# Leaving out the zero matmuls ahead of two steps of the recurrent block

## The chip, the cores and the metric

The kernel runs on one core of a Trainium2 chip. The metric is device microseconds of one execution. The core has TensorE (PE; its weight loads are PEld), VectorE (DVE), ScalarE (ACT), GpSimd (POOL) and SyncE (SP, which issues the DMAs here). Each works through its own queue in order and waits for the others on semaphores.

## What is computed

A trunk of two layers over 256 tokens of width 1024, in float32. Each layer has a combined projection, windowed attention and RWKV-7 time mixing side by side, an output projection, a product-key expert block, and a gated embedding. The change touches the time mixing. Cut to what matters:

```python
def _rwkv7_mix(f, mu, w0, w_up, a0, a_up, g_up, k_k, k_a, r_k, lnx_w, lnx_b):
    ...
    w = -jax.nn.softplus(-(w0 + jnp.tanh(xw) @ w_up)) - 0.5
    decay = jnp.exp(-jnp.exp(w.astype(jnp.float32)))
    a = jax.nn.sigmoid(a0 + xa @ a_up)
    g = jax.nn.sigmoid(xg) @ g_up
    kk = (k * k_k).astype(jnp.float32).reshape(B, S, H, N)
    kk = kk / jnp.maximum(jnp.linalg.norm(kk, axis=-1, keepdims=True), 1e-12)
    k = k * (1.0 + (a - 1.0) * k_a)
    ...
    y = _rwkv7_scan(rh, hs(decay), kh, vh, -kk, kk * ah)
    ...
    bonus = jnp.sum(rh * kh * r_k.astype(jnp.float32), axis=-1, keepdims=True)

def reference(x, p, ...):
    for i in range(DEPTH):
        h = _rmsnorm(x, norm_mix[i])
        f = h @ w_in[i] + b_in[i]
        attn = _rmsnorm(_swa_sink_attention(...), attn_out_norm[i])
        rw = _rwkv7_mix(...)
        x = x + jnp.concatenate([attn, rw], axis=-1) @ w_out[i]
        x = x + _peer(_rmsnorm(x, norm_ffn[i]), peer_wq[i], peer_keys[i], peer_u[i], peer_v[i])
        gate = jax.nn.sigmoid(_rmsnorm(x, norm_ple[i]) @ ple_gate[i])
        x = x + (p[i] @ ple_proj[i]) * gate
    return _rmsnorm(x, norm_final)
```

`kk` is the key divided by its norm over the 64 channels of a head; `a`, `g` and the decay come from small (LoRA) projections.

## The kernel before, in words

Channels lie on partitions and tokens run along the free axis. In each of the two layers, TensorE does the 21 tiles of the input projection (`channel_rows`, L1250), with the attention's matmuls between them. Then it does, in this order of its queue:

1. eight transposes of the normed attention output `ao` (L1341);
2. `keep_warm(6, 4)`: four matmuls of a tile of zeros into PSUM bank 6 (L1238);
3. a wait for `sqk`, the squared scaled keys, which ScalarE makes (L512); then two matmuls with a matrix of ones per head, the key norms' sums (L1348);
4. the LoRA matmuls for decay and `a` (L1356, L1359), a wait for ScalarE's sigmoid of the gate input (L517), and the gate matmuls (L1364, L1365);
5. a wait for `rkprod` from VectorE (L906), and two matmuls with the ones, the bonus sums (L1371);
6. the transposes to token order (L1382) of `v` (`fm[:, 8:12]`), then `keep_warm(2, 4)` into bank 2, then a wait for the scaled keys `bt` and `kt` (VectorE, L914, L915), and their transposes;
7. a wait for `ar` (L917, L918) and `bonus_v` (L920) from VectorE; 16 products, one for each half of the tokens and head, each of two matmuls (L1395, L1396). VectorE copies each out of PSUM under a mask (`prods`, L925), and from the fifth on a product waits for the copy four before it;
8. six levels of a triangular inverse: products and transposes of 128x128 blocks (L1409, L1416, L1424), with masks from GpSimd (L375, L383).

Beside this, ScalarE makes the squares, the square root of the norms (`rnorm`, L516), the sigmoids (L522, L526), the copy of the gates `gT` (L529) and three exponentials (L532, L533, L535), the last of which `bt` waits for. VectorE takes the maximum of the sums (L890), the reciprocal (L892), scans (L896), and then `cprev`, `kmod`, `rkprod`, `kk`, `bvec`, `bt`, `kt`, `ar`, `bonus_v` in this order. The order of every engine is written out by hand.

A float32 matmul leaves two records in the trace, a transpose one. So four zero matmuls are eight records, and eight transposes are eight.

Of the kernel before, what the change touches and what calls it, by code (L numbers as in the profile page):

```python
# [105 lines left out]
def hybrid_encoder(nc, x, w_slabs, peer_slabs, vecs, consts, p_t, g_final, out):  # L106
    with ExitStack() as ctx:
# [6 lines left out]
        def place(name, at, shape, dt=F32):  # L114
            return nc.alloc_sbuf_tensor_at(name, [P] + shape, dt, offset=4 * (first + at))
# [6 lines left out]
        cst = place("cst", 14336, [NCONST])  # L122
# [10 lines left out]
        zeros = place("zeros", R + 25088, [P])  # L133
# [79 lines left out]
        PS = ctx.enter_context(nc.psum_tensor("PS", [P, 8, 512], F32))  # L213
# [1009 lines left out]
        def _(pe):  # L1223
            mm = pe.matmul
# [7 lines left out]
                        if tb == TB - 1 and k % 2:  # L1232
                            ins.then_inc(xT_ps, 1)

            def keep_warm(bank, n):

                for _ in range(n):
                    mm(PS[:, bank], zeros[:], cst[:, 0:512], start=True, stop=True)  # L1238

            def channel_rows(tile, dst, norm=None):  # L1240

                pe.wait_ge(low_pool if tile.by_pool else low_dve, tile.low + 1)
                b, n = tile.count % DEEP, 0
                for k in range(KT):
                    if norm is not None:

                        pe.wait_ge(hT_lo, KT * norm + k + 1)
                    ks = slice(k * P, (k + 1) * P)
                    for w, h in ((high, hTh), (high, hTl), (low, hTh)):
                        ins = mm(dst, w[:, b, ks], h[:, k], start=n == 0, stop=n == 3 * KT - 1)  # L1250
                        n += 1
                ins.then_inc(part_used, 1)
# [19 lines left out]
            for L in range(DEPTH):  # L1272
# [66 lines left out]
                for k in range(4):  # L1339
                    for tb in range(TB):  # L1340
                        ins = pe.transpose(PS[:, AOT_BANKS[k // 2], (k % 2) * SEQ + tb * P:(k % 2) * SEQ + (tb + 1) * P], ao[:, tb, k * P:(k + 1) * P], ident)  # L1341
                    if k % 2:
                        ins.then_inc(aoT_ps, 1)
                keep_warm(6, 4)

                pe.wait_ge(sqk_ready, L + 1)
                for n in range(2):
                    ins = mm(PS[:, 6 + n], ones2, sqk[:, 2 * n:2 * n + 2].rearrange("p a b -> p (a b)"), start=True, stop=True)  # L1348
# [26 lines left out]
                pe.wait_ge(g_ready, L + 1)  # L1375
                for n, src in enumerate((fm[:, 8:12], bt, kt)):
                    if n == 1:
                        keep_warm(2, 4)
                        pe.wait_ge(bkt_ready, 2 * L + 1)
                    for tb in range(TB):  # L1380
                        for t in range(4):
                            ins = pe.transpose(PS[:, 2 * n + tb, t * P:(t + 1) * P], src[:, t, tb * P:(tb + 1) * P], ident)  # L1382
                    ins.then_inc(tok_ps, 1)
# [44 lines left out]
                for c in range(NCHUNK):  # L1428
# [6 lines left out]
                    for t in range(4):  # L1435
                        if c:
                            mm(PS[rows, 0, t * P:(t + 1) * P], ar[:, t, tb, 0, cols], ST[:, (c - 1) % 2, t], start=True, stop=False)
                        for h in (2 * t, 2 * t + 1):
                            ins = mm(PS[rows, 0, h * HD:(h + 1) * HD], prods[:, tb * NH + h, 256 + o:256 + o + 64], vtok[:, tb, h * HD:(h + 1) * HD],
                                     start=c == 0, stop=c == 0 or h % 2 == 1)  # L1440
# [249 lines left out]
```

## Time and profile before

| | us |
|---|---|
| median of three timed runs | 2381.17 (2380.63 to 2383.16) |
| profiled execution, its own time | 2383.67 |
| its span, first to last instruction | 2381.9 |
| TensorE busy | 2255.2 |
| VectorE busy | 1670.5 |
| ScalarE busy | 1118.4 |
| GpSimd busy | 472.9 |
| mean granted TensorE clock | 0.974 of full speed |

The two stretches in which the changed lines run lie at about 90 to 133 us (layer 0) and 1273 to 1317 us (layer 1). Read each in three views: the chain of waits, which tells what ended last; the timeline of each engine, which tells when an input was ready; and the windows, which tell the granted clock (PEclk, 1.00 or 0.50 of full speed) in a stretch. A time of the timeline is the start of a group and its length; the last record of a matmul group overlaps the next group a little.

### The profile page before, as it was taken

Reading aid. Unit: us, or ns where it says so; the run is one execution under the profiler, and the core shown is the slowest. Engines: PE = TensorE matmul, PEld = TensorE weight load, DVE = VectorE, ACT = ScalarE, POOL = GpSimd, SP = SyncE. Lnnn points to the kernel's source line nnn. Section 1 sums busy time; section 2 is a strip of 40 time slices with the busy share of each in tenths; the row PEclk is TensorE's granted clock in tenths of the full one; section 3 lists DMA queues with packets and bytes.
Section 4 is the critical chain, followed back from the end, with each engine's and each line's share of the span. In section 5 each row is a group of like instructions: output and inputs, shape, how many; then the busy total and the mean of one; then the engine's idle time right before and its main releaser. Section 6 shows DMA issues by size and latency. Waiting matters only on the chain.

```text
span 2381.9 us, 51888 instructions
## 1 busy us (share of the span) xinstructions
PE 2255.2 (95%) x20000; PEld 2016.4 (85%) x20000; DVE 1670.5 (70%) x3044; ACT 1118.4 (47%) x1867; POOL 472.9 (20%) x206
## 2 busy tenths in 40 slices
PE   8898899999999999999898979999899999999997
PEld 7787889998888888788686978899888888887885
DVE  6754499697666676985567555987967666679754
ACT  5532455544444444445464324554444444454443
POOL 0040379840000000000000405797400000000000
PEclk9898899999999999999998989999999999999998
DMA  6201344533444444445342013344244444444451
GB/s 245 89 1 54 117 149 158 177 123 142 159 176 159 173 161 159 159 158 194 141 142 71 1 65 130 142 176 161 105 165 170 161 174 160 175 159 150 167 194 62
DMA packets 46601, 335.02 MB, mean 141 GB/s; under 512 B 5168, under 2 KB 5296, under 8 KB 6320
## 3 DMA queue, kind: packets, MB, share of 16 engines
q1 hardware_dynamic: 46512, 333.84, 39.3%
q8 instruction: 55, 0.90, 0.2%
q14 instruction: 34, 0.28, 0.0%
HBM read 332.77 MB, written 1.05 MB: 140 GB/s over the span
## 4 chain that ended last, share of the span: by engine, by line
PE 81%; DVE 6%; issue 5%; POOL 5%; ACT 2%; DMA 1%; SPq 0%; POOLq 0%; DVEq 0%; ACTq 0%
PE PS L1542 30%; PE PS L1519 24%; PE PS L1250 7%; PE PS L1531 6%; PE PS L1266 4%; POOL low L397 4%; PE PS L1409 2%; PE PS L1416 2%; DMA praw<-in_p_t 1%; DVE is_i L1090 1%; PE PS L1424 1%; PE PS L1238 1%; DVE rnorm L892 1%; PE PS L1282 0%; PE PS L1333 0%
## 5 line engine op out<-in xcount | busy, mean ns | idle before, releaser
L600 ACT CAST high<-ring 128x1024 fp32r<-128x1024 f32 x512 | 535.5, 1048 | 609.9 <-PE PS L1519 451.0
L1519 PE MATMUL PS<-hTh,high 128*128 128x256 f32 x2048 | 594.7, 290 | 13.9 <-ACT GA L604 11.9
L1519 PE MATMUL PS<-hTh,low 128*128 128x256 f32 x2048 | 578.5, 282 | 0.0
L1519 PE MATMUL PS<-hTl,high 128*128 128x256 f32 x2048 | 576.9, 282 | 0.0
L1027 DVE TENSOR_TENSOR low<-ring,high 128x1024 fp32r<-128x1024 f32 x384 | 457.2, 1219 | 0.3
L1519 PEld LDWEIGHTS PS<-hTh,high 128*128 128x128 f32 x2048 | 387.0, 189 | 18.9 <-ACT GA L604 9.7
L1519 PEld LDWEIGHTS PS<-hTl,high 128*128 128x128 f32 x2048 | 387.4, 189 | 0.0
L1519 PEld LDWEIGHTS PS<-hTh,low 128*128 128x128 f32 x2048 | 387.3, 189 | 0.0
L397 POOL TENSOR_TENSOR low<-ring,high 128x1024 fp32r<-128x1024 f32 x128 | 345.1, 2721 | 96.8 <-ACT high L600 96.6
L1542 PE MATMUL PS<-high,WH 128*128 128x512 f32 x1024 | 323.5, 397 | 0.0
L1542 PE MATMUL PS<-low,WH 128*128 128x512 f32 x1024 | 318.0, 392 | 0.0
L1542 PE MATMUL PS<-high,WL 128*128 128x512 f32 x1024 | 316.4, 390 | 0.0
L1090 DVE TENSOR_TENSOR is_i<-iota_half,repeats 128x256 bf16<-128x256 bf16 x256 | 135.3, 529 | 252.4 <-ACT repeats L630 251.2
L360 POOL TENSOR_SCALAR stat<-stat 128x1 f32<-128x1 f32 x14 | 4.7, 334 | 1502.6 <-ACT xn L430 1502.6
L1531 PEld LDWEIGHTS PS<-hot,hot 128*128 128x128 bf16 x6144 | 170.5, 96 | 69.0 <-issue 54.1
L1542 PEld LDWEIGHTS PS<-high,WL 128*128 128x128 f32 x1024 | 192.2, 188 | 43.0
L1542 PEld LDWEIGHTS PS<-low,WH 128*128 128x128 f32 x1024 | 192.2, 188 | 42.8
L1531 PE MATMUL PS<-hot,hot 128*128 128x32 bf16 x6144 | 195.3, 177 | 15.7 <-DVE hot L1097 15.7
L1542 PEld LDWEIGHTS PS<-high,WH 128*128 128x128 f32 x1024 | 178.9, 188 | 26.4
L621 ACT CAST WH<-GA 128x256 fp32r (+1 forms) x256 | 102.7, 401 | 201.5 <-PE PS L1542 191.0
L1093 DVE TENSOR_TENSOR hot<-iota_half,repeats 128x1024 bf16<-128x1024 bf16 x256 | 179.3, 700 | 0.0
L1250 PE MATMUL PS<-hTh,high 128*128 128x256 f32 x592 | 172.7, 292 | 3.8 <-DVE hTl L787 3.6
(251 smaller groups left out, 3305.4 us busy)
## 6 DMA issues: line engine op xcount, KB each, us to landing
ring<-in_peer_slabs SPq DMA_DIRECT2D x256, 1024.0 KB, 4.8
ring<-in_w_slabs SPq DMA_DIRECT2D x58, 1024.0 KB, 4.9
xres<-in_x SPq DMA_DIRECT2D x2, 512.0 KB, 4.7
out<-obuf SPq DMA_DIRECT2D x2, 512.0 KB, 2.6
cst<-in_consts SPq DMA_DIRECT2D x1, 904.0 KB, 12.1
praw<-in_p_t SPq DMA_DIRECT2D x1, 512.0 KB, 16.7
gfin<-in_g_final SPq DMA_DIRECT2D x1, 512.0 KB, 5.7
vec<-in_vecs SPq DMA_DIRECT2D x1, 356.0 KB, 8.4
```

What stands on the lines that cost most here:

```text
L397: pool.tensor_tensor(low[:, b], ring[:, place, half * D:(half + 1) * D], high[:, b].bitcast(F32), ALU.subtract).then_inc(low_pool, 1)
L600: act.copy(high[:, (c0[L] + j) % DEEP], ring[:, place, half * D:(half + 1) * D]).then_inc(part_hi, 1)
L621: act.copy(WH[:, j % 2:j % 2 + 1], GA[:, bass.ds(place, 1)]).then_inc(w_hi, 1)
L1027: dve.tensor_tensor(low[:, b], ring[:, place, half * D:(half + 1) * D], high[:, b].bitcast(F32), ALU.subtract).then_inc(low_dve, 1)
L1090: dve.tensor_tensor(is_i2[:, b].rearrange("p t (a c) -> p t a c", c=REP), iotas[:, QT // REP * chunk:QT // REP * (chunk + 1)].unsqueeze(1) ...
L1093: dve.tensor_tensor(hot1[:, b].rearrange("p t (a c) -> p t a c", c=REP), iotas.unsqueeze(1).broadcast_to([P, GROUP, NSUB // REP, REP]), re ...
L1250: ins = mm(dst, w[:, b, ks], h[:, k], start=n == 0, stop=n == 3 * KT - 1)
L1266: ins = mm(PS[:, bank0 + 2 * tb + s], h[:, k, tb * P:(tb + 1) * P], w[:, b, s * 512:(s + 1) * 512], start=first and k == 0 and c == 0, sto ...
L1409: ins = mm(PS[:, g, (n % 4) * P:(n % 4 + 1) * P], Mt[:, lv % 2, n], X[:, n] if lv else ident, start=True, stop=True)
L1519: ins = mm(PS[:, 6 + j % 2, 0:SEQ], u[:, b, ks], h[:, k], start=n == 0, stop=n == 3 * KT - 1)
L1531: ins = mm(PS[:, 4 + b, t * QT:(t + 1) * QT], hot1[:, b, t], hot2[:, b, part, t], start=part == 0, stop=part == 2)
L1542: ins = mm(PS[:, 2 * tb + s], w[:, j % 2, tb * P:(tb + 1) * P], v[:, b, s * 512:(s + 1) * 512], start=False, stop=False, skip_group_check= ...
```

## The change

The function `keep_warm` and its two calls are removed. Each call made four matmuls of zeros into a bank that the next real matmul writes afresh. No other line is changed: the waits, the order of the queues, the buffers and the tile `zeros` (which the expert block uses to open and close its accumulation) stay as they are.

```diff
-            def keep_warm(bank, n):
-
-                for _ in range(n):
-                    mm(PS[:, bank], zeros[:], cst[:, 0:512], start=True, stop=True)
-
...
-                keep_warm(6, 4)
-
                 pe.wait_ge(sqk_ready, L + 1)
...
                     if n == 1:
-                        keep_warm(2, 4)
                         pe.wait_ge(bkt_ready, 2 * L + 1)
```

## Rows read from the trace of the kernel before

**Rows 1.** The page: busy time of TensorE, and the chain that ended last, by engine
```profile
PE 2255.2 (95%) x20000; PEld 2016.4 (85%) x20000; DVE 1670.5 (70%) x3044; ACT 1118.4 (47%) x1867; POOL 472.9 (20%) x206
...
PE 81%; DVE 6%; issue 5%; POOL 5%; ACT 2%; DMA 1%; SPq 0%; POOLq 0%; DVEq 0%; ACTq 0%
```

**Rows 2.** Chain of waits, layer 0: start us, length us, what ran (x records)
```profile
92.08 3.44 PE PS L1238 x8
...
95.52 1.73 PE PS L1348 x4
...
113.89 3.41 PE PS L1371 x4
...
118.17 3.44 PE PS L1238 x8
...
121.61 1.75 PE PS L1382 x16
...
123.36 0.64 PE PS L1395 x4
```

**Rows 3.** Chain of waits, layer 1, same columns
```profile
1297.12 3.75 PE PS L1371 x4
...
1307.18 0.64 PE PS L1395 x4
...
1309.21 0.51 PE PS L1395 x2
```

**Rows 4.** Timeline of ScalarE: start us, us, engine, line, operation, tiles, count [idle before]
```profile
93.13 1.71 ACT L512 ACTIVATE sqk<-fm,vec 128x256 f32<-128x256 f32 x4
...
109.54 1.01 ACT L529 COPY gT<-PS 128x1024 f32<-128x1024 f32 x1 [5.09 <-PE PS L1365]
...
113.78 1.04 ACT L535 ACTIVATE wprev<-cprev 128x1024 f32<-128x1024 f32 x1
...
1291.79 1.01 ACT L529 COPY gT<-PS 128x1024 f32<-128x1024 f32 x1 [4.11 <-PE PS L1365]
```

**Rows 5.** Windows: us, busy (x) of PE, PEld, DVE, ACT, POOL; PEclk; DMA share, GB/s
```profile
97.25:100.13 2.88, 2.88 (x16) 2.25 (x16) 1.73 (x2) 1.58 (x2) 0.00 (x0) 1.00 0.00 0
...
103.17:109.51 6.34, 6.34 (x12) 2.49 (x10) 6.31 (x6) 1.28 (x4) 0.00 (x0) 0.50 0.00 0
...
138.02:140.49 2.47, 0.00 (x0) 0.00 (x0) 2.47 (x1) 0.00 (x0) 2.42 (x1) 1.00 0.00 0
...
140.72:144.13 3.41, 3.41 (x18) 3.41 (x18) 3.27 (x6) 0.59 (x1) 0.00 (x0) 0.50 0.00 0
...
1198.86:1202.20 3.34, 3.08 (x25) 3.09 (x25) 3.34 (x9) 1.81 (x5) 0.00 (x0) 1.00 0.90 314
```

**Rows 6.** Timeline of TensorE, layer 0: gate matmuls, and behind the products
```profile
101.58 0.70 PE L1364 MATMUL PS<-xg_s,ring 128*128 128x256 f32 x2 [1.45 <-ACT xg_s L517]
...
104.84 1.22 PE L1364 MATMUL PS<-xg_s,ring 128*128 128x256 f32 x2
...
134.21 3.81 PE L1409 MATMUL PS<-cst,Mt 128*128 128x128 f32 x32 [1.31 <-issue]
```

**Rows 7.** Timeline of VectorE, both layers: scaled keys, bonus, masked copies of products
```profile
116.17 1.23 DVE L914 TENSOR_TENSOR bt<-bvec,winv 128x1024 f32<-128x1024 f32 x1
...
117.32 1.22 DVE L915 TENSOR_TENSOR kt<-kmod,winv 128x1024 f32<-128x1024 f32 x1
...
120.72 1.22 DVE L920 TENSOR_TENSOR bonus_v<-PS,fm 128x1024 f32<-128x1024 f32 x1
...
124.45 9.65 DVE L925 TENSOR_TENSOR prods<-PS,cst 128x512 f32<-128x512 f32 x16 [2.51 <-PE PS L1396]
...
1303.95 1.22 DVE L920 TENSOR_TENSOR bonus_v<-PS,fm 128x1024 f32<-128x1024 f32 x1
```

**Rows 8.** Timeline of TensorE: transposes of the norm that opens layer 1
```profile
1194.77 1.97 PE L1231 MATMUL PS<-cst,xn 128*128 128x128 f32 x8 [6.99 <-DVE xn L781]
...
1196.91 1.97 PE L1231 MATMUL PS<-cst,xn 128*128 128x128 f32 x8 [0.17 <-DVE xn L781]
```

## The prediction

> **What bounds the kernel now.** I read the page first: TensorE is busy 95% of the span and the chain that ended last is 81% TensorE [rows 1]. A shorter TensorE program pays only where nothing else ends at the same moment, so the views of the two stretches decide, not the share. The removed work is 16 zero matmuls (two records each), four at each place in each layer, and the chain runs through them [rows 2]. In layer 0 it goes through the first four (92.08 to 95.52) and the sums at 95.52 into work of VectorE and ScalarE that ends in `rkprod`, then through the sums of `rkprod` at 113.89, the second zero matmuls (118.17 to 121.61) and 16 transposes to the products at 123.36 [rows 2]. Layer 1 repeats this 1183.23 us later up to the sums of `rkprod` (1297.12 against 113.89), its products starting at 1307.18 [rows 2, 3]. So both places are on the path. What matters is what is late next once they are gone, and what TensorE's clock does with the gap.
>
> **First place, ahead of the key norms' sums.** The sums need `sqk`. Its four squares on ScalarE run from 93.13 to 94.84 (93.13 + 1.71) [rows 4]. Without the fill they could start at 94.87 instead of 95.52 (I allow 0.03 us from release to start): 0.65 us a layer earlier, at the most. The rest of the 3.44 us is a wait. Everything behind on the chain (`rnorm`, square root, reciprocal, scans, `kmod`, `rkprod`) moves with it one for one if its other inputs are early.
>
 A gap of 1.45 us ahead of 101.58 was followed, after 1.6 us of gate matmuls, by 0.50 from 103.17 to the last of them [rows 5, 6]. A gap of 1.31 us ahead of 134.21 cost nothing: the 32 records behind it took 3.81 us, full pace [rows 6]. The new gap is longer than all of these, so I expect the clock to fall in most executions, before or during the sums. Its bounds: the sums take 1.73 us at full clock and, by the `rkprod` sums, which have the same shape and ran at half clock, 3.41 to 3.75 [rows 2, 3]. From 94.87 they end at 96.60 (clock held) or at 98.3 (half throughout), against 97.25 now: -0.65 to +1.05 us on the VectorE chain.
>
> A second path becomes late if the clock then stays low. The LoRA matmuls have 2.88 us at full clock (97.25 to 100.13), so an estimated 5.8 at half, and the gate matmuls behind them went in 0.63 us a pair of records at full and 1.15 at half (0.70 and 1.22, less the 0.07 by which a pair overlaps the next) [rows 5, 6]; the eight pairs are 9.2 us at half. Half throughout gives 98.3 + 5.8 + 9.2 = 113.3 for the end of the gates, against 109.5 in layer 0 and 108.5 in layer 1 (1291.79, where ScalarE's copy starts, less 1183.23 and 0.03) [rows 4, 5]. ScalarE must copy the gates, load a table and make three exponentials (5.3 us, 109.54 to 113.78 + 1.04) before `bt`, which starts at 116.17: cover of 1.35 us in layer 0, and of 2.3 us in layer 1, where it starts 1.0 us earlier against the same chain [rows 4, 7]. So half throughout moves `bt` by 3.8 - 1.35 = +2.5 us in layer 0 and 4.8 - 2.3 = +2.5 in layer 1. The bounds for `bt` are therefore -0.65 and +2.5 us. In between lie the cases in which the clock falls late in the sums, or comes back with them: it was 1.00 again soon after matmuls had resumed at 140.49. None of the rows is nearer to one end, so I take the middle, +0.9 us in each layer.
>
> **Second place, ahead of the transposes of the scaled keys.** Here almost nothing is waited for. `kt` ends at 117.32 + 1.22 = 118.54 in layer 0, and TensorE reaches the fill at 118.17: the fill hides 0.4 us and delays the transposes by 3.1. The products wait also for `bonus_v` (120.72 + 1.22 = 121.94) [rows 7]. So the transposes would end at 120.3, and VectorE is late next: products at 121.98 in place of 123.36, -1.38 us. In layer 1 `bonus_v` ends at 1303.95 + 1.22 = 1305.17 [rows 7], products at 1305.20 in place of 1307.18, -1.98 us. These dates lie on the VectorE chain and move with `bt`. If the clock is still half during the 24 transposes, they take twice as long (the eight at 1194.77 took 1.97 us [rows 8]); the 16 behind `kt` then take 3.5 us instead of 1.75 [rows 2] and end at 122.0, in the shadow of `bonus_v` or 0.1 us past it.
>
> **What speaks about transposes.** The eight transposes at 1194.77 and the eight at 1196.91 took 1.97 us a group, half pace, nothing else ran on TensorE between, and the clock was 1.00 from 1198.86 [rows 5, 8]. So here transposes bring the clock back as matmuls do. The Trainium skill, in "TensorE: Matmul & The Clock Gate", Part 4 (PE-mode transpose), says the opposite, that transposes do not count as TensorE work for the clock and full clock does not engage for them. By that rule the sums of `rkprod` would be alone in restoring the clock once the fill is gone and the products would start at half clock, which is rival (c) below in both layers; the trace disagrees, and I give the rule no more than that rival's chance.
>
> **The sum.** Layer 0: +0.9 - 1.38 = -0.48. Layer 1: +0.9 - 1.98 = -1.08. Together -1.56 us. The products themselves are paced by VectorE's masked copies (16 in 9.65 us, 0.60 each [rows 7]) and, like the dense matmuls behind them, shift one for one. The profiled execution is 2383.67 us (span 2381.9 and 1.8 around it), 2.5 above the median of the three timed runs, 2381.17; from the profiled one the sum gives 2382.1, from the median 2379.6. I forecast 2379.6 us for the median. Removing instructions costs nothing elsewhere: the banks written by zeros (6 and 2) are written afresh by the next matmul, and no semaphore is tied to them.
>
> **Rivals.** (a) The clock holds in the new gap. For it: 1.31 us did no harm. Against it: the 2.47 us gap. It gives -0.65 - 1.38 in layer 0 and -0.65 - 1.98 in layer 1, -4.7 us, 2376.5. Chance 0.13. (b) The clock falls at the key norms and stays low through the gates: +2.5 - 1.4 and +2.5 - 2.0, +1.6 us, 2382.8. The gates are where the clock fell in layer 0 of before [rows 5], which speaks for it; against it, matmuls brought the clock back from 144.13. Chance 0.22. (c) The other side: the products run at half clock. The second fill ends where the transposes begin; without it, TensorE idles some 1.7 us (120.3 to 121.98) just ahead of the products. For it: the 1.45 us gap, followed by half clock. Against it: the 1.31 us gap, and sums and transposes that fill TensorE from 113.9 on. A product is four records; the first 16 (four products) of layer 1 took 2.03 us at full clock (1307.18 to 1309.21), 0.51 a product [rows 3], an estimated 1.02 at half, against the 0.60 pace of the copies: +0.42 each, 6.7 us if all 16 of a layer are so. One layer gives 2379.6 + 6.7 = 2386.3, both 2393.0. It makes the kernel slower than before from 4 such products on (1.68 us against the 1.56 gained), and by 0.2% once all 16 of one layer are so (6.7 against 6.4). Chance 0.06. (d) The clock's falls behind the products land elsewhere, such as the one at 140.72, where 3.41 us at half cost up to 1.7 us [rows 5], and shift the time by some 2 us either way with no cause at the removed lines; the three runs of before differ by 2.5 us. I put that into the width of every case.
>
> **Chances and range.** Forecast 0.55 (2377.5 to 2382), (a) 0.13, (b) 0.22, (c) 0.06, others 0.04. About 0.2%, 4.8 us, is what a measurement of this kernel can tell from no change. Faster by more than that needs (a) in both layers and luck with the later falls: 0.05. Slower needs (c): 0.06. Within: 0.89. The range reaches from (a), 2376.5, to (b) with 2 us of later falls, 2384.8: 2376.0 to 2385.0.
>
> **What would show it.** In the profile after: the key norms' sums start at about 94.9 and 1278; the granted clock at them is 0.50 in most places, and the sums take between 1.73 and 3.5 us. `bt` starts 0.65 earlier to 2.5 later than 116.17. The transposes of `bt` start when `kt` ends, and the products 0.03 to 0.1 us behind `bonus_v`, not behind TensorE. The products keep 0.60 us each. The prediction is wrong if the sums run at 1.00 in both layers, if ScalarE's exponentials are not early enough for `bt` even with a clock of 1.00, or if copies of the products stand further apart than 0.60 us.

## The result, and the profile after

The changed kernel takes 2387.76 us (median of 13 runs, 2382.24 to 2388.88) against 2381.40 for the kernel before (13 runs, 2380.28 to 2383.19). The ratio is 1.0022, with a 95% interval of 1.0014 to 1.003. So leaving work out made the kernel slower, by 6.4 us here and by 5.6 us when both were timed again (e10 below). I had forecast 2379.6, between 2376.0 and 2385.0.

The profiled execution after took 2388.56 us, its span 2386.7. Its page, the lines that answer to [rows 1] and the clock line:

```profile
PE 2258.5 (95%) x19968; PEld 2019.5 (85%) x19968; DVE 1671.4 (70%) x3044; ACT 1118.5 (47%) x1867; POOL 473.5 (20%) x206
...
PEclk9798999999999999999997989999999999999998
...
PE 80%; POOL 6%; DVE 6%; issue 6%; ACT 2%; DMA 0%; POOLq 0%; SPq 0%; DVEq 0%; ACTq 0%
```

32 matmul records are gone and TensorE is nevertheless busy for 3.3 us more: the others ran longer. The chain of waits after, layer 0, with start, length and what ran. It answers to [rows 2]; L1341 is now the line of the key norms' sums, L1357 and L1358 the gates, L1387 the products:

```profile
95.31 3.78 PE PS L1341 x4
...
104.67 1.15 PE PS L1357 x2
...
112.72 1.16 PE PS L1358 x2
...
113.91 1.01 ACT gT L529
...
118.23 0.95 ACT wprev L535
...
119.28 1.23 DVE bt L914
...
123.92 1.15 DVE bonus_v L920
...
125.19 0.71 PE PS L1387 x4
```

The chain no longer goes through VectorE's reciprocal. It goes through the LoRA and gate matmuls and ScalarE's exponentials into `bt`. The windows tell why (us, busy of PE, PEld, DVE, ACT, POOL; then PEclk; DMA share and GB/s):

```profile
95.31:99.09 3.78, 3.78 (x5) 1.24 (x5) 0.37 (x2) 1.53 (x2) 0.00 (x0) 0.50 0.00 0
99.09:104.60 5.51, 5.51 (x16) 4.11 (x16) 4.35 (x2) 4.19 (x7) 0.00 (x0) 0.50 0.00 0
104.67:113.88 9.21, 9.20 (x17) 3.92 (x16) 9.14 (x11) 1.63 (x5) 0.00 (x0) 0.50 0.00 0
115.74:121.90 6.16, 5.66 (x13) 3.09 (x14) 4.83 (x5) 4.09 (x5) 0.00 (x0) 0.50 0.34 144
125.19:135.31 10.12, 9.59 (x64) 8.26 (x64) 8.98 (x15) 0.00 (x0) 3.82 (x3) 1.00 0.01 2
1280.06:1283.85 3.79, 3.79 (x5) 1.25 (x5) 0.38 (x2) 1.53 (x2) 0.00 (x0) 0.50 0.00 0
```

From the sums to the transposes of `v` the clock is at half, in one piece; at the products it is at full. That is the mechanism of rival (b), in both layers.

It is not the whole loss. With a second trace of each kernel (e10 and e11 below) I compared the time of each stage, from the start of its first record to that of the next one's (us; two executions and two layers each, so means of four, except where a layer is named):

| stage | before | after | after - before, both layers |
|---|---|---|---|
| first transposes (L1341) to first product | 32.66 (32.27 to 32.86) | 33.25 (33.76 three times, 31.71 once) | +1.2 |
| products and inverse | 62.60 | 62.51 | -0.2 |
| chunk stage: the recurrence over four chunks, to the first transpose of `yc` | 36.30 (37.61, 35.86, 35.85, 35.86) | 37.50 (37.53, 37.43, 37.59, 37.45) | +2.4 |
| output projection, norm, start of the queries | 45.96 | 45.82 | -0.3 |
| queries, key scores | 48.10 | 47.94 | -0.3 |
| expert block | 830.13 | 830.78 | +1.3 |
| rest of layer 0 and start of layer 1 | 125.85 | 126.27 | +0.4 |
| rest of layer 1 | 52.37 | 52.47 | +0.1 |

The rows sum to +4.6, and the spans differ by 4.7 (means 2380.6 and 2385.3). Half of the loss lies in the chunk stage, no line of which was changed, 64 us behind the last removed matmul of each layer (in before, layer 0, that ends at 121.61 and the stage starts at 185.89). Its windows, layer 1, of before and then of after:

```profile
1369.70:1405.56 35.86, 29.06 (x400) 27.54 (x401) 15.63 (x27) 9.02 (x13) 0.00 (x0) 0.86 0.09 31
```

```profile
1372.38:1409.81 37.43, 30.37 (x400) 28.89 (x400) 15.63 (x27) 9.12 (x13) 0.00 (x0) 0.82 0.08 29
```

VectorE's work is the same, 15.63 us. TensorE's records are the same in number and take 1.31 us more, at a mean clock of 0.82 in place of 0.86.

### The profile page after: what moved, and what is told of

Its sections match the earlier page's. It is cut to its first block, busy times and chain, and to the rows that moved or that the text cites. A ratio compares the mean times of both kernels' runs of the same rounds, so it can differ in the third digit from the quotient of the medians.

```text
span 2386.7 us, 51824 instructions
## 1 busy us (share of the span) xinstructions
PE 2258.5 (95%) x19968; PEld 2019.5 (85%) x19968; DVE 1671.4 (70%) x3044; ACT 1118.5 (47%) x1867; POOL 473.5 (20%) x206
## 4 chain that ended last, share of the span: by engine, by line
PE 80%; POOL 6%; DVE 6%; issue 6%; ACT 2%; DMA 0%; POOLq 0%; SPq 0%; DVEq 0%; ACTq 0%
PE PS L1534 30%; PE PS L1511 22%; PE PS L1245 8%; PE PS L1523 6%; POOL low L397 5%; PE PS L1261 4%; PE PS L1401 2%; PE PS L1408 1%; DVE prods L925 1%; DVE is_i L1090 1%; PE PS L1416 1%; PE PS L1277 0%; PE PS L1328 0%; POOL Mt L383 0%; DVE hot L1097 0%
```

## The experiments

The theories that the expectations speak of, in the order in which I held them:

- **Theory 1.** The loss is a fixed cost at the first place: the clock is lost in the new gap and `bt` is late through the gates.
- **Theory 2.** It comes from the second place: the gap ahead of the products.
- **Theory 3**, formed after the first four. The first place costs and the second pays, and they nearly cancel. The larger part of the loss arises in the chunk stage, whose length depends on where in it the clock falls.

Times of before differ by up to 0.8 us between batches (2381.40, then 2380.84, 2380.81 and 2380.56), and every ratio is within its batch.

**e1, only the first fill left out.**

```diff
-                keep_warm(6, 4)
```

> Only the fill ahead of the key norms' sums is left out; the one ahead of the scaled keys' transposes stays. Theory 1 (the loss comes from the first place: the clock falls in the new gap at the key norms and stays at half until the rkprod sums, so that the scaled keys are late through the gates and ScalarE's exponentials): bt starts 2.7 us later behind the transposes at L1341 than before, as in the changed kernel, nothing of it is paid back at the second place, and the products start some 3.3 us later than before in each layer: 2388 to 2391 us, slower than the full change. Theory 2 (the loss comes from the second place, the gap of TensorE ahead of the products and what the clock does behind it): no slower than before by more than the 1.05 us a layer of the sums at half clock, 2381 to 2383.5 us.

Measured 2380.93 us (11 runs), ratio 1.0003 (0.9993 to 1.0012): no loss. Theory 1 fails as a total, by 7 us, and the time is theory 2's. Yet theory 1's mechanism is in the trace: the sums at half clock, and the products 35.20 and 35.03 us behind the first transposes, 2.9 and 2.2 later than before. What paid for it is the chunk stage, 33.18 and 31.91 us. Layer 1 of e1:

```profile
1370.20:1402.11 31.91, 24.86 (x401) 23.48 (x401) 15.63 (x27) 9.11 (x13) 0.00 (x0) 1.00 0.10 34
```

No half clock at all, and 4 to 6 us less than in before and after, for the same instructions.

**e2, only the second fill left out.**

```diff
-                        keep_warm(2, 4)
```

> Only the fill ahead of the scaled keys' transposes is left out. Theory 1: the products start 1.38 us earlier in layer 0 and 1.98 in layer 1, behind bonus_v, with the copies still 0.60 us apart: 2381.4 - 3.4 = 2378.0 us (2376.5 to 2379.5). Theory 2: the products or what stands behind them runs at half clock for longer than before, and the kernel is as slow as the full change or slower, 2386 us and up.

Measured 2379.11 us (11 runs, 2373.97 to 2382.25), ratio 0.9993 (0.9984 to 1.0002): on the side of theory 1, though not clear of no change. Theory 2 is out. In the trace the products start 31.06 us behind the first transposes in both layers, against 32.27 and 32.86: 1.2 and 1.8 us earlier, close to what was worked out. The chunk stages took 33.4 us. The execution traced is the fastest of the eleven, 5.1 us below their median, so these two chunk stages need not be those of a usual execution of e2.

**e3, three zero matmuls in place of four at the first place, none at the second.**

```diff
-                keep_warm(6, 4)
+                keep_warm(6, 3)
...
-                        keep_warm(2, 4)
```

> Three zero matmuls in place of four at the first place, none at the second. Three last 2.58 us and end at 94.66, just ahead of the squares at 94.84. Theory 1: the clock holds at 1.00 in the sums, they start 0.65 us earlier in each layer, and the kernel gains that on top of e2: 2381.4 - 3.4 - 1.3 = 2376.7 us. Theory 2: like e2, 2386 us and up.

Measured 2381.06 us (11 runs), ratio 1.0001 (0.9992 to 1.001). The clock holds in the sums and the products start at 30.70 us, 0.36 earlier than in e2 and not 0.65. The sums start 0.48 us earlier in layer 0 (3.86 us behind the first transposes against 4.34) and their first record takes 0.11 us longer. The time is not better: the chunk stages took 37.35 and 37.53 us. Windows of e3, the sums and the chunk stage of layer 1:

```profile
94.72:96.64 1.92, 1.92 (x5) 0.68 (x5) 0.38 (x2) 1.53 (x2) 0.00 (x0) 1.00 0.00 0
1364.15:1401.68 37.53, 30.47 (x401) 28.99 (x401) 15.63 (x27) 9.11 (x13) 0.00 (x0) 0.82 0.09 29
```

In these two traces an earlier stage that is 0.36 us shorter goes with a later one that is 4 us longer. The medians lie only 2 us apart, for the trace of e2 is of its fastest execution.

**e4, the changed kernel with the copy of the gates behind the exponentials** (the copy and its wait are moved).

```diff
-                act.wait_ge(lora_ps, 3 * L + 3)
-                act.copy(gT[:], PS[:, 4:6]...).then_inc(g_ready, 1)
...
                 act.activation(wprev[:], cprev[:], ACT.Exp, scale=-EXP_MINUS_HALF).then_inc(decay_ready, 1)
 
+                act.wait_ge(lora_ps, 3 * L + 3)
+                act.copy(gT[:], PS[:, 4:6]...).then_inc(g_ready, 1)
```

> The changed kernel, with ScalarE's copy of the gates moved behind its three exponentials, so that the slow gate matmuls no longer hold up the exponentials that bt needs. Theory 1, the part that says ScalarE's path through the gates ends last: bt starts directly behind bvec, 1.2 us earlier in each layer than in the changed kernel: 2387.8 - 2.5 = 2385.3 us. If the late sums on VectorE's own chain are all of the loss, the time stays at 2387.8.

Measured 2380.09 us (11 runs), ratio to before 0.9998 (0.9989 to 1.0007), 7.7 us below the changed kernel (6.0 below e10) instead of 2.5. `bt` in the timeline of VectorE, of after and then of e4:

```profile
119.28 1.23 DVE L914 TENSOR_TENSOR bt<-bvec,winv 128x1024 f32<-128x1024 f32 x1 [1.29 <-ACT wprev L535]
```

```profile
117.56 1.23 DVE L914 TENSOR_TENSOR bt<-bvec,winv 128x1024 f32<-128x1024 f32 x1
```

The wait for ScalarE is gone, and the products stand 32.50 us behind the first transposes instead of 33.76: -1.26 in each layer, as forecast. That this path ended last is shown. The traces differ by 7.3 us in all, and the other 4.8 are again no part of what was touched: 1.6 us in each chunk stage (35.84 and 35.85 for 37.5), 0.8 in each expert block (830.07 and 830.06 for 830.9), and the rest.

I now had twelve unfilled chunk stages with their clock. Sorted by how long behind the start of the stage the clock first falls:

| first fall, us behind the start | at half clock, us in all | stage, us | seen in |
|---|---|---|---|
| 2.1 to 2.6 | 13.7 | 37.35 to 37.61 | before L0, after L0 and L1, e3 L0 and L1, later e10 L0 and L1 |
| 3.0 to 3.4 | 10.2 | 35.84 to 35.86 | before L1, e4 L0 and L1, later e11 L0 and L1 |
| 4.1 | 6.8 | 34.69 | later e5 L0 |
| 4.8 | 10.2 | 36.56 | later e5 L1 |
| 5.2 | 3.4 | 33.42, 33.43 | e2 L0 and L1 |
| 20.9 | 3.4 | 33.18 | e1 L0 |
| none | 0 | 31.91 | e1 L1 |

The stage is short of work for TensorE (its waits for ScalarE's and VectorE's copies leave it idle for 0.7 to 1.7 us each). For the same instructions and the same waits it keeps the clock in one pass and loses it in another, and what it loses goes in steps of up to 2 us. First falls 0.4 us apart (2.6 and 3.0 us behind the start) went with stages 1.8 us apart. My reading, argued and not shown, was that a small shift of the stage's start against the clock's falls moves it from one step to another. The next four test this.

**e5, one zero matmul more in the changed kernel, ahead of the inverse's last level.**

```diff
+                        if lv == LEVELS - 1 and g == 0:
+                            mm(PS[:, 4], zeros[:], cst[:, 0:512], start=True, stop=True)
```

> The changed kernel with one more zero matmul of 512 columns ahead of the last level of the inverse, where TensorE is full: pure added work of some 0.86 us a layer. Theory 3 (the larger part of the loss arises in the chunk stage of the recurrence, whose length goes in steps with the instants at which the clock falls in it, and a shift of its start moves it from one step to another): the stage starts 0.86 us later against those instants, falls from 37.5 us (as in the changed kernel) to some 33.4 (as in e2), and the kernel becomes faster by 2 x 3.2: 2381.3 us. Theory 1 alone (a fixed cost at the key norms and the gates): 1.7 us slower than the changed kernel, 2389.5 us.

Measured 2386.23 us (10 runs), ratio 1.0024 (1.0015 to 1.0033). Neither number came. The stage did move to other steps, with the first fall at 4.1 and 4.8 us instead of 2.3, and 34.69 and 36.56 us, so 2.8 and 0.9 us shorter; the inverse, with the added matmul, is 0.2 and 0.9 us longer (51.84 and 52.39 us against 51.68 and 51.53). The matmul itself is 0.86 us in both layers, but in layer 0 the clock did not fall in the inverse. In that layer it had also come back in the sums, and the products stood at 32.18 us instead of 33.76. But it did not reach the 33.4 of e2, since the clock stayed low longer or fell a second time, at 32.1 us. The direction of theory 3 is seen in the stage and not in the time, and as more than the start of the stage had changed in this execution, e5 shows no more than that. The first fall's place alone doesn't fix the stage's length.

**e6, e7 and e8, the chunk stage filled,** in the changed kernel, in e2 and in the kernel before. The same three lines for each:

```diff
+                    for _ in range(1 if c else 3):
+                        mm(PS[:, 6, 0:256], zeros[:], cst[:, 0:256], start=True, stop=True)
                     pe.wait_ge(rhs_ready, NCHUNK * L + c + 1)
...
+                    mm(PS[:, 6, 0:256], zeros[:], cst[:, 0:256], start=True, stop=True)
                     pe.wait_ge(sa_ready, NCHUNK * L + c + 1)
```

> The changed kernel with zero matmuls of 256 columns in the waits of the chunk stage (three at the first wait, one at each other). Theory 3: the clock stays at 1.00 in the stage, which takes 31.9 us as in layer 1 of e1, against 37.5: 2387.8 - 11 = 2376.5 us, and the runs no longer spread over 6 us. Theory 1 alone: the stage is no part of the loss, the gain is the same as the one that the same fills give the kernel before.

> Only the second fill left out (e2), and the chunk stage filled as in e6. Theory 3: the profile of e2 had 33.4 us for the stage in both layers, so 31.9 gives 3 us there and more in the executions with the longer steps; against the kernel before with filled chunks it starts its products 1.2 and 1.8 us earlier and its inverse 0.7 us shorter in each layer: 2368 to 2371 us, faster than both kernels. Theory 1 alone: 2378 to 2380 us, like e2.

> The kernel before with the chunk stage filled as in e6. Theory 3: 37.6 and 35.9 us become 31.9, 2371 to 2374 us, and e6 minus this one shows what the change costs when the chunk stage is out of play: the 1.5 and 0.9 us by which the products start later in the two layers, 2.4 us, instead of 6.4. Theory 1 alone: e6 minus this one is 6.4 us.

| kernel | median, us | ratio to before (95%) | first product behind first transposes, L0, L1 | chunk stage |
|---|---|---|---|---|
| e6, neither fill | 2374.52 (7 runs) | 0.9971 (0.996 to 0.9983) | 33.76, 33.76 | 31.91, 31.91 |
| e7, first fill only | 2367.53 (5 runs) | 0.9945 (0.9931 to 0.9958) | 31.07, 31.06 | 31.91, 31.92 |
| e8, both fills | 2374.16 (8 runs) | 0.9973 (0.9962 to 0.9983) | 32.44, 32.80 | 31.92, 31.92 |

The chunk stage of e6, layer 0:

```profile
187.12:219.03 31.91, 30.75 (x421) 26.62 (x421) 15.63 (x27) 9.12 (x13) 0.00 (x0) 1.00 0.11 35
```

And of e8, layer 0:

```profile
185.75:217.67 31.92, 30.75 (x420) 26.61 (x420) 15.63 (x27) 9.11 (x13) 0.00 (x0) 1.00 0.11 35
```

With the clock at 1.00, the stage is 31.9 us everywhere. The changed kernel gains 12 to 13 us by it (2387.76 above, 2386.14 in e10) and the kernel before gains 7. The runs of the changed kernel also lie closer together, from 2373.01 to 2375.35 us instead of 2382.24 to 2388.88, as theory 3 said. With this stage out of play the change costs 0.4 us (e6 against e8), not 6, and the runs of the two overlap almost wholly, so this isn't told apart from nothing; the spans of the two traces differ by 0.7 us. That is less than the 2.4 I gave it: the products do start 1.3 and 1.0 us later, but the inverse gives back 0.1 and 0.2, and the expert block 0.3 and 0.4. And the two halves of the change separate. Leaving out the second fill gains 6.6 us (e8 to e7), leaving out the first then loses 7.0 (e7 to e6). e7 is 13 us faster than the kernel before and 19 to 20 than the changed one.

**e9, only the first fill left out, chunk stage filled.**

> Only the first fill left out (e1), and the chunk stage filled. Theory 3 (e1 was as fast as the kernel before only because its chunk stage fell on the short steps, 33.2 and 31.9 us, which paid for the loss at the key norms): with the chunk stage the same 31.9 us in both, the loss shows: products 2.9 and 2.2 us later than before in the two layers, 5 us slower than the kernel before with filled chunks (2374.2), 2379 us. If leaving out the first fill costs nothing by itself, it is level with that kernel, 2374.

Measured 2379.24 us (11 runs), ratio 0.9994 (0.9985 to 1.0003). It is 5.1 us slower than e8 (2374.16, in another batch whose before was 0.25 us slower), with the products 34.86 and 35.15 us behind the first transposes and 31.91 and 31.92 for the stage. So the first fill is worth 5 us beside the second and 7 without it, and e1 hid this behind a lucky chunk stage.

**e10 and e11, the two kernels unaltered, again.**

> The changed kernel unaltered, for a second trace and for times beside the other experiments. Theory 3: 2386 to 2388 us; the key norms' sums at half clock in both layers and the products 33.8 us behind the first transposes again; the chunk stage at 35.8 to 37.5 us. If the steps of the chunk stage were drawn anew in each execution, without regard to the kernel, it could as well be at 32 to 33.4.

> The kernel before unaltered, for a second trace: 2381 us. Products 32.3 to 32.9 us behind the first transposes; the chunk stage at one of the steps seen, its length set by how long behind its start the clock falls (2.6 us: 37.6; 3.2 us: 35.9; 5.2 us: 33.4).

e10 took 2386.14 us (11 runs, 2382.28 to 2388.40), ratio 1.0025 (1.0016 to 1.0034), so the loss holds. e11, one run, took 2381.12. Chunk stages of e10, and then of e11:

```profile
1369.54:1406.99 37.45, 30.39 (x401) 28.92 (x401) 15.63 (x27) 9.12 (x13) 0.00 (x0) 0.82 0.09 29
184.81:222.40 37.59, 30.53 (x401) 29.05 (x401) 15.63 (x27) 9.12 (x13) 0.00 (x0) 0.82 0.09 29
```

```profile
186.29:222.14 35.85, 29.06 (x400) 27.54 (x400) 15.62 (x27) 9.01 (x13) 0.00 (x0) 0.86 0.09 31
1367.47:1403.33 35.86, 29.06 (x400) 27.54 (x401) 15.63 (x27) 9.01 (x13) 0.00 (x0) 0.86 0.09 31
```

After has 37.4 to 37.6 in all four passes, before has 35.9 in three of four. So the steps aren't drawn without regard to the kernel. They aren't fixed by it either: layer 0 of before took 37.61 us in one execution and 35.85 in the other, and the eleven runs of e2 spread over 8.3 us. The executions of the changed kernel fall into two groups by their mean granted clock: 0.967 to 0.969 with 2387.4 to 2388.9 us (8 of the first 13 runs, 5 of the 11 of e10), and 0.971 to 0.973 with 2382.2 to 2386.2 us (5 and 6). The first profile is of the slower group, e10's of the faster. Layer 0 of e10 is the one pass in which the clock fell late in the sums (2.93 us instead of 3.7), and its products stood at 31.71 us, 0.65 later than in e2, whose clock held.

**e12, three zero matmuls at the first place, chunk stage filled.**

> e7 with three zero matmuls in place of four at the first place. e3's trace started the products 0.36 us earlier than e2's, and the chunk stage is now out of play: 0.7 us faster than e7, 2366.8 us. If the shorter fill loses the clock it is slower by up to 7 us, as e6 against e7.

Measured 2367.58 us (5 runs, 2364.22 to 2369.54), ratio 0.9948 (0.9934 to 0.9961): level with e7. The 0.7 us are in the trace (products at 30.70 us) but below what five runs tell apart.

## Why the prediction was wrong, step by step

**What bounds the kernel, and where the removed work lay: right.** Both fills are on the chain, and after the change the chain goes on without them.

**First place, "I take the middle, +0.9 us in each layer": wrong, and the first step that failed.** The upper bound, +2.5 us for `bt`, was nearly right: the profile after has +2.7, that is 119.28 - 91.44 = 27.84 us behind the first transposes against 116.17 - 91.02 = 25.15. The first transposes of before and of after:

```profile
91.02 1.06 PE L1341 MATMUL PS<-cst,ao 128*128 128x128 f32 x8 [0.61 <-issue]
```

```profile
91.44 1.06 PE L1336 MATMUL PS<-cst,ao 128*128 128x128 f32 x8 [0.61 <-issue]
```

The lower bound, -0.65, was too large a gain. It took the sums' old start from the chain, 95.52, where the timeline has 95.36, and e3, where the clock holds, brought the products forward by 0.36.

The clock fell at the key norms or just ahead of them in all 14 passes traced without the first fill, and in none of the 14 with it (whole, or three matmuls of it). The sums took 3.7 us in 12 of them, 3.4 and 2.9 in the others. I had reasoned that the clock would come back with the sums, as it came back at 144.13 [rows 5]. It did not, in 12 of 14: the LoRA matmuls (64 of the 128 rows of the array) and the gate matmuls (every other pair with 32 rows) follow the sums, and the clock stayed at 0.50 through 5.5 and 9.2 us of them. It came back at or behind the `rkprod` sums and the transposes behind them, which use all rows. Before had pointed to this too: it is the gate matmuls in which the clock stayed low from 103.17 to 109.51 [rows 5], though TensorE was busy for all of it. That was the row nearest to the case, and the 140.72 one, with full-height matmuls behind the gap, was not. The term should have been the upper end, with rival (b) as the likeliest case: 2382.8 by its own sum, still 5 us short of what was measured. In the other two passes, layer 0 of e10 and of e5, the middle case did occur: the clock came back 1.3 us into the LoRA matmuls (e10) or near the end of the sums (e5), and the products stood at 31.71 and 32.18 us.

That the few rows are the cause isn't shown, for no run changed them. Against it stand the LoRA matmuls of before, which ran at full clock behind the fill (97.25 to 100.13 [rows 5]), and the gate matmuls in layer 0 of e10, which ran at full clock throughout.

The sentence "Slower needs (c): 0.06" fails with this step. The kernel became slower by 6.4 us and (c) did not occur.

**Second place: right in mechanism, short in size.** The products now wait for `bonus_v`, and start 1.2 and 1.8 us earlier in e2 (1.38 and 1.98 forecast). With the chunk stage filled the removal is worth 6.6 us rather than 3.36. Of the rest, 1.4 is in the inverse, which was 50.98 us in both layers of e7 and 51.68 in those of e8. That is the fall of the clock at 140.72 [rows 5]: it is gone in e2, e3, e7 and e12, which all have 50.98, and its 3.41 us at half clock cost 0.7 us and not 1.7. Another 1.0 is in the expert blocks (829.93 and 829.89 against 830.40 and 830.38), and 0.7 in the rest of layer 1 behind it (51.74 us against 52.42).

**Rival (c), the products at half clock: did not occur.** They run at 1.00 after (125.19 to 135.31), and the copies stand 0.60 us apart. 24 transposes lay ahead of them, 8 of these behind the `rkprod` sums at half clock. The rule of the Trainium skill that the prediction weighed ("TensorE: Matmul & The Clock Gate", Part 4, that transposes do not engage full clock) would have given this rival by the prediction's own working, and the products came out at full clock. But this is no second test of the rule: 3.75 us of `rkprod` sums stand ahead of the transposes, and in before, layer 0, the clock rose within those sums (at 116.82; they run from 113.89 to 117.30), so here the sums can have brought it back alone.

**Rival (d), "shift the time by some 2 us either way ... I put that into the width of every case": wrong in kind, and the step that cost most.** Of the difference between the sum and the traces, 2.8 us arise up to the first product (-1.56 forecast, +1.2 measured) and 3.4 behind it. I had seen that the clock's falls behind the change cost time, and took them for noise that favours neither kernel. But in part they go with the kernel: half of the +4.7 us between the spans is the chunk stage. A quarter is the expert block, whose fall near its middle lasted longer in the profile after (mean clock from 540 to 555 us of 0.77, against 0.89). First before, then after:

```profile
540.00:555.00 15.00, 12.20 (x153) 11.29 (x152) 10.25 (x18) 5.28 (x10) 0.00 (x0) 0.89 0.36 128
```

```profile
540.00:555.00 15.00, 12.25 (x131) 11.31 (x130) 10.39 (x18) 4.30 (x9) 0.00 (x0) 0.77 0.32 114
```

That difference belongs to the kernel only in part. The fall lasted 6.8 us in all four passes of after, but in before it lasted 3.4 us in two passes and 6.8 in the other two. Over all traces the block took 829.8 to 830.1 us with a fall of 3.4 us there and 830.3 to 831.0 with one of 6.8.

The chunk stage alone can give 31.9 to 37.6 us in each layer, 11 us in all, against the 1.56 that I had summed. Its share of half clock stood in the trace of before and I gave it no term.

**What stays open.** Why the same kernel mostly meets the same step. In layer 1 the clock fell 2.65 to 2.90 us behind the first transposes in all seven traces without the first fill, and 12.85 to 13.35 us behind them in six of the seven with it (16.51 in e3). So the clock's falls and the kernel's work keep nearly the same distance in separate executions. A stage that runs at half clock until the clock rises ends at a time that partly depends on that rise, which would pull executions together; this is argued and not shown. e5's steps, 34.7 and 36.6, were not foreseen, so the table of steps can't yet be used to predict a kernel. And each kernel has one trace, before and after two, so what stage took the time in an execution that wasn't traced is not known.

## What to carry to other kernels

In these runs a fill of zero matmuls earned its place where the work behind the gap was matmuls with 64 or 32 rows, through which the clock in these traces stayed at half; it was waste where transposes and sums already stood around a gap of 0.4 us. When a change shifts a kernel by a microsecond, list every later stage in which TensorE's granted clock is below 1.00 and ask what it would cost if that share changed: here they made nearly three quarters of the loss between the traces (3.4 of 4.6 us). Fill such a stage first (13 and 7 us for three lines); only then do small edits measure as what they are.

## What the runs showed of the hardware

- The same 400 records of the chunk stage took 31.91 us at a mean clock of 1.00 and 37.5 at 0.82, and filling the waits with 20 records of zeros added nothing to 31.9.
- The fall of the clock in the inverse, 3.41 us at half, cost that stage 0.5 to 1.0 us: it took 50.98 us in the eight passes without such a fall and 51.5 to 52.0 in the others (e5 left out, which has a matmul more).
- Behind an idle stretch of 0.22 us the first record of the sums took 0.70 us instead of 0.59 (e3 against e2), at full clock in both.
